# Row statistics of the input norm: sums of squares on TensorE from a ring of four buffers, with the tokens split at column 520

## The chip, the cores and the metric

The kernel runs on one core of a Trainium2 chip. The metric is device time in microseconds (us), the median of several executions; lower is better. The engines are TensorE (PE, with its weight loads PEld), VectorE (DVE), ScalarE (ACT), GpSimd (POOL) and SyncE (SP), which mostly issues DMAs.

## What is computed

One inference step of a one-layer hybrid decoder trunk: 1024 prompt tokens and 8 sample tokens share the weights, and 256 memory tokens have a projection of their own. The change is in the first norm, whose rows are the tokens:

```python
def rmsnorm(x, g):
    xf = x.astype(jnp.float32)
    y = xf * lax.rsqrt(jnp.mean(xf * xf, axis=-1, keepdims=True) + EPS)
    return (y * g.astype(jnp.float32)).astype(x.dtype)

z = rmsnorm(x, g) @ w_in          # prompt and sample tokens, in project()
z = rmsnorm(mem, g) @ w           # memory tokens, in memory_kv()
```

The columns of `z` feed four groups (forgetting attention, spatial gating, dilated attention, memory attention); then come the output projection, a residual add and a ConvFFN. All of that is untouched.

## The kernel before

The input lies transposed, features on the 128 partitions and tokens along the columns: 8 sample columns, then 1024 prompt columns (`COLS` = 1032), in `KC` = 8 chunks of 128 features. A product in full precision is made of three matmuls: both operands are split into a high and a low part (`hhi`, `hlo` for x times the gain; `whi`, `wlo` for the weights), and hi*hi, hi*lo and lo*hi are summed in PSUM (L903 to L905). ACT makes the high parts (`x_hi` L1228, `split_hi` L1220), DVE the low ones (`x_lo` L1622, `split_lo` L1616). The projection of x doesn't wait for the row statistics: 1/rms of a token is applied when the tile of `z` is moved out of PSUM.

The work of this stage is a list of units (L272): `(5, 0)` and `(5, 1)` are the two tiles of memory tokens against `w_mem`; then for each of five column blocks b of `w_in` come `(b, "S")`, whose first 8 columns are the sample tokens, and the eight prompt tiles `(b, 0)` to `(b, 7)`. A unit is 8 groups (kc) of three matmuls, 24 in all, and every engine's program walks the same list in its own order.

x comes in 24 pieces, i = 0 to 23, in three thirds of 8 (`xwhere` L296): memory tokens, the first 516 columns, the last 516. A piece is loaded by SP into one of seven slots (`x_load` L501; piece i waits until x_lo and the square of piece i-7 are done). ACT makes the high part (`x_hi`), and then the square of the piece (`x_square` L1236). For i = 0 to 15 ACT's order is x_hi(i), split_hi(i), x_square(i); pieces 16 to 23 come in `second_half` (L1263), which stands ahead of the eviction of unit (0,"S").

The statistics before: the square of the first piece of a third goes to `sacx`, the others go to `sqt0` and `sqt1` in turn, and POOL adds each of these to `sacx` (`x_add` L2314), 21 adds in all. A square waits until POOL has used the buffer (`x_acc`). When a third is complete, PE sums `sacx` over the partitions: a matmul per tile of 128 tokens, whose stationary operand is the 128x128 tile of `sacx` and whose moving operand is one column of ones (`stats` L816: 2, 4 and 5 matmuls, after units (5,0), (0,"S") and (0,2)). The second third also waits for `rtab` (made by `tables` L1592 on DVE) and for `st_cp`; with it go six small matmuls for the gains and then `page_transposes` (L834). DVE copies the sums out (`stat_copy` L1608) and POOL makes the inverse root (`inverse_rms` L2307, `rs_row`). POOL's own order is: 8 x_add, first inverse_rms, two indirect DMAs for `lfp`, a mask, 8 x_add, inverse_rms for tiles S, 0, 1, 2, 8 x_add, and from there two small instructions for each unit that is normed.

An eviction goes ACT square (L1312), DVE sum (L1672), POOL inverse root (L2310, L2313), DVE scale (L1685, L1692). DVE's `second_half` (L1638: copy of the sums, x_lo of pieces 16 to 23, a scan over `lft` L1647 and a subtraction L1649) stands in front of the eviction of (0,"S"). Prompt units take PSUM banks 0 to 3 in turn, so (0,4) waits for the eviction of (0,0), and so on. SP stores finished tiles (`outputs` L520); at unit (0,4) it waits for the normed sample rows, then moves q to `qb`, and then issues sixteen times two page loads for the key cache (`load_pages` L361), with the stores and the weight loads of the later blocks queued behind them.

Of the kernel before, what the change touches and what calls it, by code (L numbers as in the profile page):

```python
# [33 lines left out]
BLK = [(0, 512), (512, 260), (772, 512), (1284, 512), (1796, 512)]  # L34
ATT, DIL, MEMG = 0, 1, 2
NSET = 12

# [60 lines left out]
def build(nc, t):  # L98
# [5 lines left out]
    with ctx:  # L104
# [19 lines left out]
        u10_0 = cur[0]  # L124
# [44 lines left out]
        lft = at("lft", [P, 2, NH, P], f32, u10_0)[0]  # L169
        lmask = at("lmask", [P, 2 * NH * P], f32, pidx_end)[0]  # L170
        lscan = at("lscan", [P, 2 * NH * P], f32, 224416)[0]
        sqt1 = at("sqt1", [P, 516], f32, pidx_end + 4096)[0]
        rtab = at("rtab", [4, NR], f32, 224416)[0]
        relb = at("relb", [32, NH], f32, 224416 + 4608)[0]

# [22 lines left out]
        zs, o = at("zs", [NSAMP, 2308], f32, o)  # L198
        sA, o = at("sA", [P, 8, PAGES, NH], f32, o)
        accx = at("accx", [NSAMP, 2, NH, HD], f32, o - 4096)[0]  # L200
        sacx, sq_end = at("sacx", [P, COLS], f32, o - 4096)
        sqt0 = at("sqt0", [P, 516], f32, u10_0 + 4096)[0]
        lfp = at("lfp", [P, 2, PSZ * NH], f32, sq_end)[0]
        bias0 = o
        biasA, o = at("biasA", [P, 8, PAGES, NH], f32, o)
        oS = at("oS", [NSAMP, 4, WG], f32, bias0)[0]
        qb, o = at("qb", [P, 8, WG], f32, o)
        ring, o = at("ring", [P, 4, 4, WG], f32, o)
        x7 = at("x7", [P, 7, 516], f32, o - 16384)[0]
        coh = at("coh", [32, NR + 320], f32, bias0 + 4096 + 1024)[0]  # L210
        wost1 = at("wost1", [P, KC, P], f32, o)[0]
        wost0 = at("wost0", [P, KC, P], f32, u10_0)[0]
# [82 lines left out]

        def xwhere(i):  # L296

            c0, w = ((516, NMEM), (0, 516), (516, 516))[i // 8]
            return slice(c0, c0 + w), w, i % 8, 1 if i < 8 else 0

        def xslot(i):

            return x7[:, i % 7, 0:xwhere(i)[1]]

        def xsem(i):
            return S(f"x_ld{i % 7}")
# [484 lines left out]
        def _(pe):  # L791
# [10 lines left out]

            pe.wait_ge(S("const_ld"), 80)

            def stats(half):

                pe.wait_ge(S("x_acc"), 8 * half + 8)
                if half:
                    pe.wait_ge(S("rtab"), 4)
                    pe.wait_ge(S("st_cp"), half)  # L810
                cols = ([(9 + x, 516 + x * P) for x in range(2)],
                        [(0, 0)] + [(1 + tt, NSAMP + tt * P) for tt in range(3)],
                        [(1 + tt, NSAMP + tt * P) for tt in range(3, NT)])[half]
                if half == 1:

                    for j in range(3):  # L816
                        for r0 in (0, HD):
                            pe.matmul(ps[r0:r0 + HD, 7, 300 + j:301 + j], gq[0:1, 2 * j, :], ones[0:1, 0:1], start=True, stop=True)
                for x, c0 in cols:
                    m = pe.matmul(ps[:, 7, 288 + x:289 + x], sacx[:, c0:c0 + P], ones[:, 0:1], start=True, stop=True)  # L820
                m.then_inc(S("st_pe"), 1)

            def page_transposes():

# [49 lines left out]
            for u, k in enumerate(units):  # L874
# [13 lines left out]
                        pe.wait_ge(S("dve_z"), dve_last(pk))  # L888
                elif bank[k] in (2, 3):
                    pe.wait_ge(S("rtab"), 4)  # L890
                c0 = 0 if tt == "S" else (516 + tt * P if b == 5 else NSAMP + tt * P)
                for kc in range(KC):
                    if tt == "S" or (b == 5 and tt == 0):
                        pe.wait_ge(S("w_split"), POS[b] * KC + kc + 1)
                    if b == 0:
                        pe.wait_ge(S("x_split"), KC + kc + 1 if tt in ("S", 0, 1, 2) else 2 * KC + kc + 1)
                    if b == 5:
                        pe.wait_ge(S("x_split"), kc + 1)
                    sl = (POS[b] * KC + kc) % NW
                    w = WID[b]  # L900
                    lh, ll = hhi[:, kc, c0:c0 + P], hlo[:, kc, c0:c0 + P]
                    out = ps[:, bank[k], 0:w]
                    pe.matmul(out, lh, whi[:, sl, 0:w], start=(kc == 0), stop=False)  # L903
                    pe.matmul(out, lh, wlo[:, sl, 0:w], start=False, stop=False)  # L904
                    i = pe.matmul(out, ll, whi[:, sl, 0:w], start=False, stop=(kc == KC - 1))  # L905
                    if tt == NT - 1 or (b == 5 and tt == 1):
                        i.then_inc(S("w_used"), 1)
                    elif kc == KC - 1:
                        i.then_inc(S("z_done"), 1)
                if tt == NT - 1 or (b == 5 and tt == 1):  # L910

                    pe.wait_ge(S("w_used"), (POS[b] + 1) * KC)
                    pe.sem_inc(S("z_done"), 1)
                if k == (5, 0):
                    stats(0)
                if k == (0, "S"):
                    stats(1)
                    page_transposes()
                if k == (0, 2):
                    stats(2)  # L920
                if k == (0, 4):
                    page_sums()
                if k == (2, 1):
# [295 lines left out]
        def _(act):  # L1219
# [15 lines left out]

            def x_square(i):  # L1236

                c, w, kc, _ = xwhere(i)
                if kc == 0:
                    if i == 2 * KC:  # L1240
                        act.wait_ge(S("st_pe"), 1)
                    act.activation(sacx[:, c], xslot(i), ACT.Square).then_inc(S("x_sq"), 1)
                else:
                    if i >= 3:
                        act.wait_ge(S("x_acc"), i - 1)
                    act.activation((sqt0 if i % 2 else sqt1)[:, 0:w], xslot(i), ACT.Square).then_inc(S("x_sq"), 1)
            act.dma_start(relb[:, :], t["rel_bias"]).then_inc(S("tab_ld"), 16)
            act.dma_start(coh[:, :], t["coh"]).then_inc(S("tab_ld"), 16)
            act.dma_start(ca[:, :], t["ca"]).then_inc(S("const_ld"), 16)
# [34 lines left out]
            for u, k in enumerate(units):  # L1284
# [5 lines left out]
                r = rows(k)  # L1290
                rx = rsx[0:r, xi(k):xi(k) + 1]
                z = zview(k)
                act.wait_ge(S("rs_row"), 1 if b == 5 else 2 if u < UI[(0, 3)] else 3)
                act.wait_ge(S("z_done"), u + 1)
                dst = zdst(k)
                if b in COPY or b == 2:
# [281 lines left out]
        def _(dve):  # L1578
# [28 lines left out]

            def stat_copy(half):  # L1608

                a, b = ((9, 11), (0, 4), (4, 9))[half]  # L1610
                dve.wait_ge(S("st_pe"), half + 1)
                if half == 1:
                    dve.tensor_copy(ssx[:, 11:14], ps[:, 7, 300:303])
                dve.tensor_copy(ssx[:, a:b], ps[:, 7, 288 + a:288 + b]).then_inc(S("st_cp"), 1)
# [13 lines left out]
            for kc in range(KC):  # L1628
                x_lo(kc)
                split_lo(kc)  # L1630
            stat_copy(0)
            for kc in range(KC, 2 * KC):
                x_lo(kc)
                split_lo(kc)
            dve.wait_ge(S("const_ld"), 80)
# [667 lines left out]
        def _(pool):  # L2303
# [3 lines left out]
            def inverse_rms(out, src, width, done, value):  # L2307
# [3 lines left out]
                chain[0] += 1  # L2311
                pool.wait_ge(S("pool_chain"), chain[0])
                pool.tensor_tensor(out, out, nhalf[0:r, 0:n], ALU.pow).then_inc(S(done), 1)  # L2313
            def x_add(i):  # L2314

                c, w, _, _ = xwhere(i)
                pool.wait_ge(S("x_sq"), i + 1)
                if i % 8 == 0:
                    pool.sem_inc(S("x_acc"), 1)
                    return  # L2320
                if i % 8 > 1:
                    pool.wait_ge(S("x_acc"), i)
                pool.tensor_tensor(sacx[:, c], sacx[:, c], (sqt0 if i % 2 else sqt1)[:, 0:w], ALU.add).then_inc(S("x_acc"), 1)

            for i in range(KC):
                x_add(i)
            pool.wait_ge(S("st_cp"), 1)
            inverse_rms(rsx[:, 9:11], ssx[:, 9:11], DM, "rs_row", 1)
            pool.wait_ge(S("const_ld"), 80)
            for i in range(2):  # L2330
# [3 lines left out]

            pool.affine_select(out=wsT[:, :, :], in_=wsT[:, :, :], compare_op=ALU.is_ge, fill=0.0, base=0,
                               pattern=[[0, NH], [1, P]], channel_multiplier=-1).then_inc(S("ws_mask"), 2)
            for i in range(KC, 2 * KC):
                x_add(i)
            for u, k in enumerate(units):
                if k == (0, "S"):  # L2340
                    pool.wait_ge(S("st_cp"), 2)
                    inverse_rms(rsx[:, 0:4], ssx[:, 0:4], DM, "rs_row", 2)
                    for i in range(2 * KC, 3 * KC):
                        x_add(i)
                if k == (0, 3):
                    pool.wait_ge(S("st_cp"), 3)
                    inverse_rms(rsx[:, 4:9], ssx[:, 4:9], DM, "rs_row", 3)
# [98 lines left out]
```

## Time and profile before

| | |
|---|---|
| median of 3 runs | 1478.48 us |
| lowest, highest | 1466.24, 1486.55 us |
| the profiled execution | 1470.2 us, span of its instructions 1468.5 us |
| PE busy | 1402.7 us, 96% of the span |
| DVE busy | 942.8 us, 64% |
| ACT busy | 463.4 us, 32% |
| POOL busy | 186.3 us, 13% |
| mean granted TensorE clock | 0.965 of full speed |

Times in the rows are us from the span's start. The stage that the change touches is the first 100 us or so; the projections end near 297, attention near 520, and the rest is the output projection and the ConvFFN, where PE is busy nearly all the time.

### The profile page before, as it was taken

Reading aid. Unit: us, or ns where it says so; the run is one execution under the profiler, and the core shown is the slowest. Engines: PE = TensorE matmul, PEld = TensorE weight load, DVE = VectorE, ACT = ScalarE, POOL = GpSimd, SP = SyncE. Lnnn points to the kernel's source line nnn. Section 1 sums busy time; section 2 is a strip of 40 time slices with the busy share of each in tenths; the row PEclk is TensorE's granted clock in tenths of the full one; section 3 lists DMA queues with packets and bytes.
Section 4 is the critical chain, followed back from the end, with each engine's and each line's share of the span. In section 5 each row is a group of like instructions: output and inputs, shape, how many; then the busy total and the mean of one; then the engine's idle time right before and its main releaser. Section 6 shows DMA issues by size and latency. Waiting matters only on the chain.

```text
span 1468.5 us, 24237 instructions
## 1 busy us (share of the span) xinstructions
PE 1402.7 (96%) x8753; PEld 1271.9 (87%) x8753; DVE 942.8 (64%) x1412; ACT 463.4 (32%) x711; POOL 186.3 (13%) x245
## 2 busy tenths in 40 slices
PE   6899999969898999999999999999999999999999
PEld 4678887756665666899999999999999999999999
DVE  6758889876676685744765646556564746465654
ACT  6413121164455555522432222122222212121220
POOL 5540024332221243000000000000000000000000
PEclk9899999987888799999999999999999999999999
DMA  8248766687875776341001202020201102020203
GB/s 280 56 143 262 221 179 186 186 234 214 255 237 184 250 219 178 94 154 29 29 29 58 72 15 72 15 87 1 87 29 58 58 29 72 15 72 15 81 7 127
DMA packets 125536, 168.62 MB, mean 115 GB/s; under 512 B 22789, under 2 KB 99998, under 8 KB 125010
## 3 DMA queue, kind: packets, MB, share of 16 engines
q1 hardware_dynamic: 100988, 129.44, 28.6%
q0 software_dynamic: 7616, 22.03, 5.1%
q10 hardware_dynamic: 16814, 15.62, 3.5%
q8 instruction: 69, 1.13, 0.3%
q14 instruction: 49, 0.40, 0.1%
HBM read 153.09 MB, written 13.96 MB: 114 GB/s over the span
## 4 chain that ended last, share of the span: by engine, by line
PE 77%; DVE 9%; issue 4%; POOL 3%; DMA 2%; SPq 2%; ACT 1%; ACTq 1%; POOLq 0%; DVEq 0%
PE ps L1106 18%; PE ps L1105 18%; PE ps L1107 18%; PE ps L1003 4%; PE ps L1028 2%; PE ps L985 2%; PE ps L903 2%; PE ps L970 2%; PE ps L904 2%; PE ps L905 2%; POOL rsn L2313 1%; PE ps L969 1%; PE ps L1007 1%; PE ps L871 1%; DVE hlo L1625 1%
## 5 line engine op out<-in xcount | busy, mean ns | idle before, releaser
L1105 PE MATMUL ps<-hhi,uhi 128*128 128x344 f32 x1056 | 338.0, 320 | 0.0
L1106 PE MATMUL ps<-hlo,uhi 128*128 128x344 f32 x1056 | 336.5, 319 | 0.0
L1107 PE MATMUL ps<-hhi,ulo 128*128 128x344 f32 x1056 | 336.3, 318 | 0.0
L1105 PEld LDWEIGHTS ps<-hhi,uhi 128*128 128x128 f32 x1056 | 198.2, 188 | 0.5 <-issue 0.5
L1106 PEld LDWEIGHTS ps<-hlo,uhi 128*128 128x128 f32 x1056 | 198.2, 188 | 0.5 <-issue 0.5
L1107 PEld LDWEIGHTS ps<-hhi,ulo 128*128 128x128 f32 x1056 | 198.2, 188 | 0.0
L2222 DVE TENSOR_TENSOR uu<-ps,rstd_bc 128x1032 f32<-128x1032 f32 x44 | 54.2, 1233 | 202.4 <-PE ps L1107 202.2
L903 PE MATMUL ps<-whi,hhi 128*128 128x512 f32 (+1 forms) x376 | 145.9, 388 | 13.5 <-DVE wlo L1619 8.3
L1106 PE MATMUL ps<-alo,dhi 128*128 128x344 f32 x480 | 153.9, 321 | 0.0
L1107 PE MATMUL ps<-ahi,dlo 128*128 128x344 f32 x480 | 153.2, 319 | 0.0
L1105 PE MATMUL ps<-ahi,dhi 128*128 128x344 f32 x480 | 153.1, 319 | 0.0
L905 PE MATMUL ps<-whi,hlo 128*128 128x512 f32 (+1 forms) x376 | 143.1, 381 | 0.0
L904 PE MATMUL ps<-wlo,hhi 128*128 128x512 f32 (+1 forms) x376 | 142.7, 379 | 0.0
L2255 DVE TENSOR_TENSOR x<-ps,x 128x1032 f32<-128x1032 f32 x80 | 98.5, 1231 | 19.1 <-PE ps L1107 18.9
L1003 PEld LDWEIGHTS ps<-vst,pts 128*128 128x128 f32 x576 | 74.8, 204 | 30.5 <-issue 27.7
L903 PEld LDWEIGHTS ps<-whi,hhi 128*128 128x128 f32 x376 | 72.5, 193 | 31.7 <-DVE wlo L1619 12.3
L365 POOL DMA_DIRECT2D vring<-in_cache_a_v x128 | 70.0, 547 | 183.4 <-issue 143.5
L1523 ACT ACTIVATE convG<-uu,prm_a 128x1024 f32<-128x1024 f32 x22 | 27.4, 1244 | 201.9 <-DVE uu L2222 201.9
L1107 PEld LDWEIGHTS ps<-ahi,dlo 128*128 128x128 f32 x480 | 90.2, 188 | 0.0
L1105 PEld LDWEIGHTS ps<-ahi,dhi 128*128 128x128 f32 x480 | 90.1, 188 | 0.0
L1106 PEld LDWEIGHTS ps<-alo,dhi 128*128 128x128 f32 x480 | 90.1, 188 | 0.0
L1003 PE MATMUL ps<-vst,pts 128*128 128x65 f32 x576 | 82.9, 293 | 6.2 <-DVE oN L1960 5.9
(291 smaller groups left out, 2412.9 us busy)
## 6 DMA issues: line engine op xcount, KB each, us to landing
fst<-in_w_upL SPq DMA_DIRECT2D x44, 512.0 KB, 3.5
ring<-in_cache_a_k SPq DMA_DIRECT2D x168, 128.0 KB, 2.6
vring<-in_cache_a_v POOLq DMA_DIRECT2D x128, 128.0 KB, 3.3
vring<-in_cache_a_v SPq DMA_DIRECT2D x104, 128.0 KB, 3.0
ring<-in_cache_a_k ACTq DMA_DIRECT2D x88, 128.0 KB, 2.8
fst<-in_w_down SPq DMA_DIRECT2D x22, 512.0 KB, 3.5
wst<-in_w_in SPq DMA_DIRECT2D x32, 256.0 KB, 3.7
x<-in_xT SPq DMA_DIRECT2D x16, 258.0 KB, 3.7
```

What stands on the lines that cost most here:

```text
L365: sp.dma_start(dst[:, slot, j, :], pool[bass.ds(page, 1)].rearrange("o p c -> p (o c)"))\
L903: pe.matmul(out, lh, whi[:, sl, 0:w], start=(kc == 0), stop=False)
L904: pe.matmul(out, lh, wlo[:, sl, 0:w], start=False, stop=False)
L905: i = pe.matmul(out, ll, whi[:, sl, 0:w], start=False, stop=(kc == KC - 1))
L970: i = pe.matmul(out, q1c[0:K2, p, q0:q0 + P], klc[0:K2, p, c:c + w], start=False, stop=True)
L985: i = pe.transpose(ps[:, 4, j * P:(j + 1) * P], lg[:, g % 2, j * P:(j + 1) * P], ident)
L1003: i = pe.matmul(ps[:, 6, 0:HD + 1], pts[:, g % 2, j, :], vst[:, hp % 2, j, H % 2, :], start=(j == 0), stop=(j == nb - 1))
L1105: pe.matmul(out, lhs_hi(kc), rhs_hi(kc)[:, cs], start=(n == 0), stop=False)
L1106: pe.matmul(out, lhs_hi(kc), rhs_lo(kc)[:, cs], start=False, stop=False)
L1107: i = pe.matmul(out, lhs_lo(kc), rhs_hi(kc)[:, cs], start=False, stop=(n == nk - 1))
L2222: dve.tensor_tensor(c3(uu[:, :]), U3(k % 2), c3(rstd_bc[:, :]), ALU.mult).then_inc(S("f_free"), 1)
L2255: dve.tensor_tensor(c3(x2[:, d, :]), U3(d % 2), c3(x2[:, d, :]), ALU.add).then_inc(S("f_free"), 1)
```

## The change

Every square goes into one of four buffers (`sqt0`, `sqt1` and the two halves of a new `sqt2`, where `sacx` was), and PE sums each piece over the partitions as soon as it is there, accumulating over the eight pieces of a third in PSUM. POOL's adds are gone. `x_acc` is now counted by PE, once for each piece, and the square of piece i waits for the sums of piece i-4. The pieces of the first third are summed inside unit (5,0), behind each group of three matmuls; those of the second inside (0,"S"), the last behind it; those of the third behind (0,0), (0,1) and (0,2), 3, 3 and 2 pieces. The second third now is 520 columns (sample tokens and tiles 0 to 3) and the last one 512. So the sums of tile 3 come with the second third, and the wait for the third moves from (0,3) to (0,4). `stat_copy(0)` on DVE is moved behind two more pieces.

```diff
+XH = 520
-            c0, w = ((516, NMEM), (0, 516), (516, 516))[i // 8]
+            c0, w = ((XH, NMEM), (0, XH), (XH, COLS - XH))[i // 8]
+        def xsquare(i):
+            s4 = i % 4
+            return (sqt0, sqt1)[s4] if s4 < 2 else sqt2[:, s4 - 2]
...
-            def stats(half):
-                pe.wait_ge(S("x_acc"), 8 * half + 8)
-                if half:
+            def stats(i):
+                half = i // KC
+                cols = ([(9 + x, x * P) for x in range(2)],
+                        [(0, 0)] + [(1 + tt, NSAMP + tt * P) for tt in range(4)],
+                        [(1 + tt, NSAMP + tt * P - XH) for tt in range(4, NT)])[half]
+                if i % KC == 0 and half:
+                    pe.wait_ge(S("st_cp"), half)
+                if i == 2 * KC - 1:
                     pe.wait_ge(S("rtab"), 4)
...
+                pe.wait_ge(S("x_sq"), i + 1)
                 for x, c0 in cols:
-                    m = pe.matmul(ps[:, 7, 288 + x:289 + x], sacx[:, c0:c0 + P], ones[:, 0:1], start=True, stop=True)
-                m.then_inc(S("st_pe"), 1)
+                    m = pe.matmul(ps[:, 7, 288 + x:289 + x], xsquare(i)[:, c0:c0 + P], ones[:, 0:1],
+                                  start=(i % KC == 0 and x == cols[0][0]), stop=(i % KC == KC - 1 and x == cols[-1][0]))
+                m.then_inc(S("x_acc"), 1)
...
+                    if k == (5, 0):
+                        stats(kc)
+                    if k == (0, "S") and kc < KC - 1:
+                        stats(KC + kc)
...
-                if k == (5, 0):
-                    stats(0)
                 if k == (0, "S"):
-                    stats(1)
+                    stats(2 * KC - 1)
                     page_transposes()
-                if k == (0, 2):
-                    stats(2)
+                if b == 0 and tt in (0, 1, 2):
+                    for x in range(2 * KC + 3 * tt, min(2 * KC + 3 * tt + 3, 3 * KC)):
+                        stats(x)
...
             def x_square(i):
-                c, w, kc, _ = xwhere(i)
-                if kc == 0:
-                    if i == 2 * KC:
-                        act.wait_ge(S("st_pe"), 1)
-                    act.activation(sacx[:, c], xslot(i), ACT.Square).then_inc(S("x_sq"), 1)
-                else:
-                    if i >= 3:
-                        act.wait_ge(S("x_acc"), i - 1)
-                    act.activation((sqt0 if i % 2 else sqt1)[:, 0:w], xslot(i), ACT.Square).then_inc(S("x_sq"), 1)
+                w = xwhere(i)[1]
+                if i >= 4:
+                    act.wait_ge(S("x_acc"), i - 3)
+                act.activation(xsquare(i)[:, 0:w], xslot(i), ACT.Square).then_inc(S("x_sq"), 1)
...
-                act.wait_ge(S("rs_row"), 1 if b == 5 else 2 if u < UI[(0, 3)] else 3)
+                act.wait_ge(S("rs_row"), 1 if b == 5 else 2 if u < UI[(0, 4)] else 3)
...
-            stat_copy(0)
             for kc in range(KC, 2 * KC):
+                if kc == KC + 2:
+                    stat_copy(0)
                 x_lo(kc)
                 split_lo(kc)
...
-            def x_add(i):
-
-                c, w, _, _ = xwhere(i)
-                pool.wait_ge(S("x_sq"), i + 1)
-                if i % 8 == 0:
-                    pool.sem_inc(S("x_acc"), 1)
-                    return
-                if i % 8 > 1:
-                    pool.wait_ge(S("x_acc"), i)
-                pool.tensor_tensor(sacx[:, c], sacx[:, c], (sqt0 if i % 2 else sqt1)[:, 0:w], ALU.add).then_inc(S("x_acc"), 1)
-
-            for i in range(KC):
-                x_add(i)
```

The two other calls of `x_add` on POOL go too, and its inverse roots take columns 0 to 4 and 5 to 8 in place of 0 to 3 and 4 to 8; `stat_copy` does the same and waits for `x_acc` at 8, 16 and 24.

## Rows read from the trace of the kernel before

**Rows 1.** Waits of PE, 0 to 330: for whom, total, times, longest.
```profile
PE ps L903 <- DVE wlo L1619: 8.3, 6, 2.8
PE ps L871 <- DVE zo L1685: 4.6, 1, 4.6
PE ps L903 <- issue: 4.3, 1, 4.3
```
**Rows 2.** Timeline, POOL's adds and ACT's squares waiting: start, us, engine, line; idle before.
```profile
27.71 11.28 POOL L2323 TENSOR_TENSOR sacx<-sacx,sqt 128x516 f32<-128x516 f32 x7
29.05 0.64 ACT L1246 ACTIVATE sqt<-x 128x516 f32<-128x516 f32 x1 [4.43 <-POOL sacx L2323]
49.63 0.64 ACT L1246 ACTIVATE sqt<-x 128x516 f32<-128x516 f32 x1 [8.97 <-POOLq L2319]
```
**Rows 3.** Timeline, ACT's pace, and DVE's splits beside POOL's adds and after them.
```profile
31.25 0.71 ACT L1234 ACTIVATE hhi<-x,prm_a 128x516 fp32r<-128x516 f32 x1
32.91 0.71 ACT L1234 ACTIVATE hhi<-x,prm_a 128x516 fp32r<-128x516 f32 x1
34.40 1.77 DVE L1619 TENSOR_TENSOR wlo<-wst,whi 128x512 fp32r<-128x512 f32 x1
36.09 1.77 DVE L1625 SCALAR_TENSOR_TENSOR hlo<-x,prm_a,hhi 128x516 fp32r<-128x516 f32 x1
39.47 0.74 DVE L1625 SCALAR_TENSOR_TENSOR hlo<-x,prm_a,hhi 128x516 fp32r<-128x516 f32 x1
40.13 0.68 DVE L1619 TENSOR_TENSOR wlo<-wst,whi 128x512 fp32r<-128x512 f32 x1
```
**Rows 4.** Timeline of PE, the marks of its order.
```profile
12.23 0.80 PE L903 MATMUL ps<-whi,hhi 128*128 128x512 f32 x1
12.82 0.63 PE L904 MATMUL ps<-wlo,hhi 128*128 128x512 f32 x1
13.25 0.63 PE L905 MATMUL ps<-whi,hlo 128*128 128x512 f32 x1
26.96 0.47 PE L903 MATMUL ps<-whi,hhi 128*128 128x512 f32 x1 [0.30 <-PE ps L905]
44.73 1.19 PE L829 MATMUL ps<-ca,lfp 128*128 128x128 f32 x8
45.67 0.48 PE L903 MATMUL ps<-whi,hhi 128*128 128x512 f32 x1
75.07 0.77 PE L903 MATMUL ps<-whi,hhi 128*128 128x512 f32 x1 [4.25 <-issue]
83.07 1.02 PE L837 MATMUL ps<-lft,ca 128*128 128x512 f32 x2
86.11 0.79 PE L903 MATMUL ps<-whi,hhi 128*128 128x512 f32 x1
134.15 0.51 PE L903 MATMUL ps<-whi,hhi 128*128 128x512 f32 x1 [1.17 <-DVE wlo L1619]
```
**Rows 5.** Timeline of PE, what stands beside the one-column matmuls of L820.
```profile
20.23 0.40 PE L905 MATMUL ps<-whi,hlo 128*128 128x512 f32 x1
20.47 0.50 PE L820 MATMUL ps<-ca,sacx 128*128 128x1 f32 x4
20.83 0.48 PE L903 MATMUL ps<-whi,hhi 128*128 128x512 f32 x1
...
63.76 0.39 PE L905 MATMUL ps<-whi,hlo 128*128 128x512 f32 x1
63.99 1.17 PE L820 MATMUL ps<-ca,sacx 128*128 128x1 f32 x10
65.02 0.47 PE L903 MATMUL ps<-whi,hhi 128*128 128x512 f32 x1
```
**Rows 6.** Timeline, the chain from the eviction of (0,"S") to SP.
```profile
66.80 0.68 DVE L1672 TENSOR_REDUCE ssn<-sq 8x8 f32<-8x512 f32 x1 [0.80 <-ACT sq L1312]
83.37 0.32 SPq L536 DMA_DIRECT2D scr_q<-zo  x1
```
**Rows 7.** Stretches: us, PE busy (instructions), granted clock, DMA share, GB/s.
```profile
45.00:48.00 3.00, 3.00 (x15) 0.69 0.14 53
75.00:78.00 3.00, 2.93 (x7) 0.50 0.18 47
436.00:440.00 4.00, 4.00 (x27) 1.00 1.12 356
```
**Rows 8.** Timeline of PE in attention, narrow matmuls at either clock.
```profile
437.26 0.39 PE L976 MATMUL ps<-khh,qhl 128*128 128x256 f32 x1
437.57 0.38 PE L977 MATMUL ps<-klc,qhl 64*128 64x256 f32 x1
437.88 1.10 PE L1007 MATMUL ps<-vst,pts 128*128 128x65 f32 x8
454.75 1.97 PE L1007 MATMUL ps<-vst,pts 128*128 128x65 f32 x8
460.42 1.11 PE L1007 MATMUL ps<-vst,pts 128*128 128x65 f32 x8
```

More of the change, by code:

```diff
@@ L171, in build @@
         lscan = at("lscan", [P, 2 * NH * P], f32, 224416)[0]
-        sqt1 = at("sqt1", [P, 516], f32, pidx_end + 4096)[0]
+        sqt1 = at("sqt1", [P, XH], f32, pidx_end + 4096)[0]
         rtab = at("rtab", [4, NR], f32, 224416)[0]
@@ L200, in build @@
         accx = at("accx", [NSAMP, 2, NH, HD], f32, o - 4096)[0]
-        sacx, sq_end = at("sacx", [P, COLS], f32, o - 4096)
-        sqt0 = at("sqt0", [P, 516], f32, u10_0 + 4096)[0]
+        sqt2, sq_end = at("sqt2", [P, 2, XH], f32, o - 4096)
+        sqt0 = at("sqt0", [P, XH], f32, u10_0 + 4096)[0]
         lfp = at("lfp", [P, 2, PSZ * NH], f32, sq_end)[0]
@@ L208, in build @@
         ring, o = at("ring", [P, 4, 4, WG], f32, o)
-        x7 = at("x7", [P, 7, 516], f32, o - 16384)[0]
+        x7 = at("x7", [P, 7, XH], f32, o - 16384)[0]
         coh = at("coh", [32, NR + 320], f32, bias0 + 4096 + 1024)[0]
@@ L803, in _ @@
             pe.wait_ge(S("const_ld"), 80)
-            def stats(half):
-                pe.wait_ge(S("x_acc"), 8 * half + 8)
-                if half:
-                    pe.wait_ge(S("rtab"), 4)
[L810 to L814, printed above, removed]
+            def stats(i):
[6 more added lines that the diff above has]
+                if i == 2 * KC - 1:
+                    pe.wait_ge(S("rtab"), 4)
                     for j in range(3):
                         for r0 in (0, HD):
-                            pe.matmul(ps[r0:r0 + HD, 7, 300 + j:301 + j], gq[0:1, 2 * j, :], ones[0:1, 0:1], start=True, stop=True)
+                            pe.matmul(ps[r0:r0 + HD, 7, 300 + j:301 + j], gq[0:1, 2 * j, :], ones[0:1, 0:1], start=False, stop=False)
+                pe.wait_ge(S("x_sq"), i + 1)
                 for x, c0 in cols:
-                    m = pe.matmul(ps[:, 7, 288 + x:289 + x], sacx[:, c0:c0 + P], ones[:, 0:1], start=True, stop=True)
-                m.then_inc(S("st_pe"), 1)
+                    m = pe.matmul(ps[:, 7, 288 + x:289 + x], xsquare(i)[:, c0:c0 + P], ones[:, 0:1],
+                                  start=(i % KC == 0 and x == cols[0][0]), stop=(i % KC == KC - 1 and x == cols[-1][0]))
+                m.then_inc(S("x_acc"), 1)
             def page_transposes():
@@ L890, in _ @@
                     pe.wait_ge(S("rtab"), 4)
-                c0 = 0 if tt == "S" else (516 + tt * P if b == 5 else NSAMP + tt * P)
+                c0 = 0 if tt == "S" else (XH + tt * P if b == 5 else NSAMP + tt * P)
                 for kc in range(KC):
@@ L895, in _ @@
                     if b == 0:
-                        pe.wait_ge(S("x_split"), KC + kc + 1 if tt in ("S", 0, 1, 2) else 2 * KC + kc + 1)
+                        pe.wait_ge(S("x_split"), KC + kc + 1 if tt in ("S", 0, 1, 2, 3) else 2 * KC + kc + 1)
                     if b == 5:
@@ L1608, in stat_copy @@
             def stat_copy(half):
-                a, b = ((9, 11), (0, 4), (4, 9))[half]
-                dve.wait_ge(S("st_pe"), half + 1)
+                a, b = ((9, 11), (0, 5), (5, 9))[half]
+                dve.wait_ge(S("x_acc"), KC * (half + 1))
                 if half == 1:
@@ L2336, in _ @@
                                pattern=[[0, NH], [1, P]], channel_multiplier=-1).then_inc(S("ws_mask"), 2)
-            for i in range(KC, 2 * KC):
-                x_add(i)
             for u, k in enumerate(units):
@@ L2341, in _ @@
                     pool.wait_ge(S("st_cp"), 2)
-                    inverse_rms(rsx[:, 0:4], ssx[:, 0:4], DM, "rs_row", 2)
-                    for i in range(2 * KC, 3 * KC):
-                        x_add(i)
+                    inverse_rms(rsx[:, 0:5], ssx[:, 0:5], DM, "rs_row", 2)
                 if k == (0, 3):
                     pool.wait_ge(S("st_cp"), 3)
-                    inverse_rms(rsx[:, 4:9], ssx[:, 4:9], DM, "rs_row", 3)
+                    inverse_rms(rsx[:, 5:9], ssx[:, 5:9], DM, "rs_row", 3)
                 if k == units[NU - 1]:
```

## Prediction, made before the changed kernel was built or run

> **What bounds the kernel now.** The page gives PE 96% of the span, so the question for each stage is what keeps PE from starting its next unit. I read the waits of PE first, then the timeline around each wait, then the stretches for the granted clock. In the first 300 us PE stands still in three ways that could concern the change [rows 1]. It waits six times for the low part of the weights, 8.3 us in all, nearly all inside unit (0,"S"). It waits 4.3 us once for "issue": that is unit (0,4) at 75.07, held by the eviction of (0,0) [rows 4]. The 4.6 us at the end of the projections are one more eviction that is late, and belong to the stage behind.
>
> The first two have one root, POOL. Its seven adds of the second third take 11.28 us, and ACT's square of piece 11 stood 4.43 us behind them; the one of piece 18 stood 8.97 us behind POOL's place in its order [rows 2]. While POOL adds, DVE's splits take 1.77 us, and 0.74 and 0.68 us once it has stopped [rows 3]: DVE is slowed 2.4 times. So the reader should see two costs of the adds, the wait for them and the slowing of DVE beside them. From 75 us on PE waits only 1.17 us until the projections end, at 134.15 [rows 4], for weights that SP issued late. So two clocks run to that point: PE's own, and SP's, which starts with the store of (0,2) at 83.37 [rows 6].
>
> **What the change adds to PE.** The one-column matmuls are 11 now and become 16 + 40 + 32 = 88. Each is two instructions, since the rows count 10 for five. Ten of them between two neighbours of 0.23 us spacing cost 65.02 - 63.76 - 0.23 = 1.03 us, four cost 20.83 - 20.23 - 0.23 = 0.37 us [rows 5]. So one statistic is 0.206 us when five stand together and 0.185 us in pairs, and the 77 added ones cost near 77 x 0.2 = 15.6 us of PE time. Of them 14 lie in (5,0), 36 in (0,"S") and 27 behind (0,0) to (0,2).
>
> The Trainium skill ("TensorE: Matmul & The Clock Gate", section "Back-to-back issue gap") lists about 62 ns for a matmul of 1 to 64 columns when its firmware decodes it; an estimate by that is 154 x 0.062 = 9.5 us, some 6 us less than by the rows. The measured spacing here, 103 ns, has a weight load of 128 columns in front of every such matmul, so I go by the measurement.
>
> **What it removes, step by step, as PE's new timeline.**
> (5,0) starts at 12.2 as before. It ended at 20.47, with about 1.4 us of waits for DVE that disappear behind the added work: 19.1. Added are 8 x 0.37 = 3.0 us, and 0.5 us more because the first groups run at half speed (spacing 0.43 us [rows 4]): 22.6. The bare kernel was at 20.83 there [rows 5]; PE is 1.8 us late.
> (5,1) and the step to (0,"S") took 26.96 - 20.83 = 6.1 us [rows 4, 5]: (0,"S") starts at 28.7.
> (0,"S") now is 7 groups of 0.70 + 1.03 = 1.73 us and one of 0.70: 12.8 us, end at 41.5. It is no longer DVE that sets it: without POOL's adds a pair of splits is 0.74 + 0.68 = 1.4 us [rows 3], below 1.73. ACT is coupled to PE here: the square of piece 12 needs the sums of piece 8, which PE only makes at 29.7 + 1 us, so a wait of about 4 us stays on ACT, at another place, and pieces 13 to 15 then come at PE's pace. Queued behind that square are x_hi and split_hi of piece 13, which PE needs at 28.7 + 5 x 1.73 = 37.4; they are there by 33. The wait costs nothing.
> Behind it come the gain matmuls and the last five sums, 0.5 + 1.0 us, and the page transposes, 0.9 us (44.73 to 45.67 [rows 4]). DVE's tables, which ran 2.5 us behind its last split (40.8 to 43.3), now follow at about 36 and end by 39, and the page rows have long landed, since POOL issues them at about 25 to 29. (0,0) starts at 44.0, against 45.67: 1.6 us won.
> (0,0) to (0,2) took 18.3 us, of which 16.8 are 72 spacings of 0.233; the rest was half clock, 0.69 granted in 45:48 [rows 7]. Now 16.8 + 32 x 0.206 = 23.4 us: 67.4. (0,3) adds 5.6: 73.0, against 70.6 before. Here PE is 2.4 us behind.
> But the 4.3 us wait goes, and the half clock after it, 0.50 in 75:78 [rows 7], which cost about 2.2 us (11 spacings at 0.43 instead of 0.23). ACT's square 23 waits for the first sums behind (0,1), at 58.5, so the eviction of (0,"S") is summed at about 60.0 instead of 66.8 [rows 6]. With the pace of 4 us per unit as before, (0,0) is out at 68, five us before (0,4) asks for its bank. (0,4) takes 5.6 us and the page sums 3.05 (83.07 to 86.11 [rows 4]): (0,5) starts at 81.7 against 86.11 [rows 4]. PE is 4.4 us ahead.
> At 134.15 the 1.17 us wait also goes if SP is early enough. SP's chain starts with the store of (0,2), 6.8 us earlier by the same shift, so PE's 4.4 + 1.2 = 5.6 us is the smaller and decides.
>
> **Where I choose.** The sum is -5.6 us with full clock all along. The narrow stretch behind (0,"S"), 2.4 us of one-column matmuls and transposes, is there in both kernels, and the clock fell around it before (0.69 in 45:48 with PE busy 3.00 of 3.00 us [rows 7]). A fall costs about 1.6 us of dense matmuls. I count one, there or behind the sums of (0,0) or (0,1): -4 us. Against the profiled execution that is 1468.5 - 4 = 1464.5 us of span; the profiled run is 8 us below the median of the three, and against the median the forecast is 1478.5 - 4 = 1474.5 us. The costs that no row shows are small: the fourth buffer, the width 520 instead of 516 (below 1% of 0.7 us, 8 times), and the three inverse roots with one column moved. After the projections every queue starts from the end of the last unit, so the gain goes through; attention has DMA-fed waits whose phase can turn 2 us either way.
>
> **Rivals.**
> (A) The forecast: a small gain, -2 to -7 us. Chance 0.55.
> (B) The clock, on the other side. TensorE's clock falls to its lower level, 1.2 GHz, inside (0,"S"), where only 0.70 of each 1.73 us is wide matmuls. A group is then 3 x 0.43 + 10 x 0.2 = 3.3 us (narrow matmuls double too: eight of 65 columns took 1.97 us at the low and 1.11 at the high clock [rows 8]). Eight groups: 12.5 us more, net +7: 1485 us. For it: the fall at 45 to 48 with a busy PE. Against it: 436:440 in attention, granted 1.00 [rows 7], where four matmuls of 256 columns and eight of 65 alternate [rows 8], with no more wide work than here. It turns the sign when four of the eight groups run low. Chance 0.2.
> (C) A wash, within 2 us: the clock falls two or three times behind the blocks of sums, or DVE and POOL's ping-pong of evictions holds (0,4) anyway. About 1478 us. Chance 0.15.
> (D) The sums are cheaper than their rows. If the weight loads hid behind the wide neighbours, a sum of pairs would fall from 0.37 towards 0.12 us, and two thirds of 15.6 us would be back; ACT then binds at 1.66 us a piece (31.25 to 32.91 [rows 3]), and the gain is about -10 us: 1468. The skill's figure in the sentence above points this way, the two rows with neighbours against it. Chance 0.1.
> That leaves the case that POOL's adds were no cost, because ACT still waits for piece 12: it is in C, since DVE's slowing goes in any case.
>
> **How the numbers follow.** All cases lie within 1% of the time; 2% is 30 us, about what a measurement of this kernel can tell from no change, and no mechanism above reaches it in either direction. The runs before spread over 20 us, more than all cases, so the range is the cases widened by some of that: 1463 to 1486, which holds A to most of B. Faster by over 2%: 0.02, within 2%: 0.95, slower: 0.03.
>
> **What would show it.** Right: no POOL adds, splits of DVE at 0.7 us throughout, L903 in (0,"S") every 1.7 us without waits for wlo, a square of ACT waiting some 4 us for PE near 26 to 30, (0,4) with no wait near 73, (0,5) near 82, and the first wide matmul after 130 without a wait. Wrong: a granted clock of 0.5 between 29 and 42 (B); a wait for an eviction at (0,4) or (0,5) (C); a pair of sums well below 0.37 us (D); or a new wait for the weights in (0,"S") although POOL is idle, which would mean that DMA and not DVE was late.

## The result and the profile after

The changed kernel is slower: 1485.95 us (median of 21 runs) against 1471.91 us for the kernel before (21 runs). The ratio is 1.0075, with a 95% interval of 1.0044 to 1.0105; it leaves out the few slow executions of either kernel. By the ratio the loss is 11 us, by the two medians 14.0 us, in a direction that I gave one chance in five. The profiled execution has a span of 1490.9 us against 1468.5.

Where it goes can be read off three marks on PE, the starts of the page transposes (behind unit (0,"S")), of the page sums (behind (0,4)) and of the first key transposes (the end of the projections). They stand at 44.7, 83.1 and 284.7 us before, and at 60.4, 99.3 and 299.5 us after. The loss of 16 us is complete at the first mark, inside the stage that the change touches, and 14.8 us of it are left at the last. The other 7.7 us between the two profiled executions lie in attention (from the first key transposes to the output projection, 371.3 us after and 363.6 before). What comes behind attention takes 820.1 to 820.7 us in all profiles of this document.

The waits of PE, 0 to 330 us, beside [rows 1]:

```profile
PE ps L878 <- DVE zo L1691: 4.8, 1, 4.8
PE ps L1094 <- DVE nm L1943: 1.3, 1, 1.3
PE ps L995 <- ACT lg L1373: 0.7, 1, 0.7
PE ps L910 <- PE ps L912: 0.6, 2, 0.3
PE ps L910 <- DVE fa L1715: 0.3, 1, 0.3
PE ps L858 <- PE ps L912: 0.3, 1, 0.3
PE ps L910 <- DVE wlo L1624: 0.3, 1, 0.3
```

Both waits of the forecast are gone: 8.3 us for the low part of the weights have become 0.3, and unit (0,4) waits for nobody. A reader who went by waits alone would call this a success. The stretches tell the other half (us, PE busy and instructions, granted clock, DMA share, GB/s). Kernel after:

```profile
12.00:30.00 18.00, 18.00 (x62) 1.00 0.77 248
30.00:45.00 15.00, 14.70 (x73) 0.93 0.59 183
45.00:63.00 18.00, 18.00 (x79) 0.50 0.12 31
63.00:100.00 37.00, 37.00 (x185) 0.95 0.27 81
```

Kernel before, the same stretches:

```profile
12.00:30.00 18.00, 17.12 (x66) 1.00 0.93 304
30.00:45.00 15.00, 7.85 (x34) 0.66 0.45 138
45.00:63.00 18.00, 18.00 (x76) 0.91 0.24 68
```

PE is busy 18.00 of 18.00 us in 45:63, at half clock. The column for the clock says 1.00 for 12:30, although the spacing of the matmuls below is that of the low level; in the kernel before, too, it says 1.00 for 12:15, where the spacing is 0.43 us [rows 4]. So ahead of the first rise the level has to be read from the spacing. Timeline of PE after, a group of (5,0), a group of (0,"S") before the fall and one behind it:

```profile
19.03 0.77 PE L910 MATMUL ps<-whi,hhi 128*128 128x512 f32 x1
19.60 0.63 PE L911 MATMUL ps<-wlo,hhi 128*128 128x512 f32 x1
20.03 0.63 PE L912 MATMUL ps<-whi,hlo 128*128 128x512 f32 x1
20.46 0.85 PE L826 MATMUL ps<-ca,sqt 128*128 128x1 f32 x4
21.16 0.77 PE L910 MATMUL ps<-whi,hhi 128*128 128x512 f32 x1
...
37.99 1.17 PE L826 MATMUL ps<-ca,sqt 128*128 128x1 f32 x10
39.02 0.48 PE L910 MATMUL ps<-whi,hhi 128*128 128x512 f32 x1
...
43.76 2.13 PE L826 MATMUL ps<-ca,sqt 128*128 128x1 f32 x10
45.75 0.77 PE L910 MATMUL ps<-whi,hhi 128*128 128x512 f32 x1
46.32 0.63 PE L911 MATMUL ps<-wlo,hhi 128*128 128x512 f32 x1
46.75 0.63 PE L912 MATMUL ps<-whi,hlo 128*128 128x512 f32 x1
47.18 2.13 PE L826 MATMUL ps<-ca,sqt 128*128 128x1 f32 x10
49.16 0.77 PE L910 MATMUL ps<-whi,hhi 128*128 128x512 f32 x1
```

The spacing of the wide matmuls in (5,0) is 0.43 us, the lower level of 1.2 GHz, up to 32.4 us, well into (5,1); in the kernel before it became 0.23 us at about 15.4. So a group of (5,0) takes 21.16 - 19.03 = 2.13 us all the way. In (0,"S") ten narrow instructions cost 39.02 - 37.99 = 1.03 us at the high level, the term of my sum, and 45.75 - 43.76 = 1.99 us at the low one. The level falls at 43 and comes back at 63, in (0,0), where the wide matmuls stand alone again.

### The profile page after: what moved, and what is told of

The parts are those of the page before. It is cut to its first block, busy times and chain, and to the rows that moved or that the text cites. A ratio compares the mean times of both kernels' runs of the same rounds, so it can differ in the third digit from the quotient of the medians.

```text
span 1490.9 us, 24503 instructions
## 1 busy us (share of the span) xinstructions
PE 1436.5 (96%) x8907; PEld 1307.6 (88%) x8907; DVE 931.5 (62%) x1412; ACT 465.3 (31%) x711; POOL 158.0 (11%) x224
## 4 chain that ended last, share of the span: by engine, by line
PE 84%; DVE 7%; issue 4%; DMA 2%; POOL 1%; ACT 1%; ACTq 1%; SPq 0%; POOLq 0%; DVEq 0%
PE ps L1116 18%; PE ps L1115 18%; PE ps L1117 18%; PE ps L1013 4%; PE ps L910 4%; PE ps L911 3%; PE ps L912 3%; PE ps L1038 2%; PE ps L995 2%; PE ps L826 2%; PE ps L980 2%; PE ps L1017 1%; PE ps L979 1%; PE ps L878 1%; DVE ring L1663 1%
```

## The experiments

The marks of all profiles, in us, with the medians and the ratios to the kernel before on the same chip (that kernel's median was 1471.91 to 1479.44 us, by chip):

| kernel | page transposes | page sums | end of projections | median | ratio (95%) |
|---|---|---|---|---|---|
| before | 44.7 | 83.1 | 284.7 | | |
| after | 60.4 | 99.3 | 299.5 | 1485.95 | 1.0075 (1.0044 to 1.0105) |
| after_again | 59.8 | 100.7 | 300.8 | 1489.17 (a single execution) | |
| e1_block | 51.4 | 92.2 | 292.3 | 1488.23 | 1.0050 (1.0000 to 1.0100) |
| e2_filler | 55.8 | 93.3 | 293.4 | 1483.59 | 1.0061 (1.0025 to 1.0097) |
| e3_nosum | 36.3 | 67.5 | 267.7 | 1458.02 | 0.9892 (0.9852 to 0.9933) |
| e4_split | 46.4 | 80.7 | 283.3 | 1471.44 | 1.0016 (0.9977 to 1.0055) |
| e5_dve | 39.4 | 71.1 | 273.5 | 1469.12 | 0.9975 (0.9940 to 1.0011) |
| e5_again | 39.5 | 71.2 | 274.0 | 1469.34 | 0.9934 (0.9875 to 0.9992) |
| e6_f32r | 39.4 | 71.8 | 272.1 | 1459.34 | 0.9917 (0.9875 to 0.9959) |
| e6_again | 39.0 | 71.5 | 271.8 | 1478.14 (a single execution) | |
| e7_row | 36.9 | 70.5 | 271.6 | 1461.44 | 0.9917 (0.9879 to 0.9955) |
| e8_double | 59.9 | 100.5 | 300.8 | 1490.51 | 1.0054 (0.9999 to 1.0108) |

The marks repeat within 1.4 us between two executions of one kernel, the totals of one kernel scatter by 15 to 32 us. So mechanisms are judged by the marks and versions by the ratios.

Theory 1 is that the one-column matmuls between the wide ones cost twice: their own 0.1 us an instruction, and the clock of everything around them. Theory 2, the rival, is that the added instructions alone cost the time.

**e1_block, the sums of (5,0) behind the unit.**

```diff
+            buf = (sqt0, sqt1)[s4] if s4 < 2 else sqt2[:, s4 - 2]
+            return buf[:, 256 * (i // 4):256 * (i // 4) + 256] if i < KC else buf
...
-                if i >= 4:
-                    act.wait_ge(S("x_acc"), i - 3)
+                if i >= KC:
+                    act.wait_ge(S("x_acc"), max(KC, i - 3))
...
-                    if k == (5, 0):
-                        stats(kc)
...
+                if k == (5, 0):
+                    for x in range(KC):
+                        stats(x)
```

> The changed kernel, but the sums of the first third stand in one block behind unit (5,0) and not behind each of its groups (the four buffers hold two 256-column pieces each, so ACT is not held back). Same matmuls, same order of everything else. Theory 1 (the narrow matmuls between the wide ones keep TensorE at its low level in (5,0)): the clock rises near 15 us as in the kernel before, (5,0) with its sums ends near 23 instead of 29.7, (0,"S") starts near 29 instead of 37.2, (0,0) near 54 instead of 62.0, time some 8 us below the changed kernel. Theory 2 (the place of the sums is indifferent, the added instructions as such cost the time): (0,"S") starts at 37 as before, time unchanged.

Timeline of PE in e1_block:

```profile
17.07 0.63 PE L912 MATMUL ps<-wlo,hhi 128*128 128x512 f32 x1
...
18.04 0.40 PE L912 MATMUL ps<-wlo,hhi 128*128 128x512 f32 x1
...
20.37 0.39 PE L913 MATMUL ps<-whi,hlo 128*128 128x512 f32 x1
20.60 3.63 PE L827 MATMUL ps<-ca,sqt 128*128 128x1 f32 x32
24.08 0.48 PE L911 MATMUL ps<-whi,hhi 128*128 128x512 f32 x1
...
25.19 0.63 PE L911 MATMUL ps<-whi,hhi 128*128 128x512 f32 x1
```

With the same instructions, the wide ones first, the level is high from about 17.5 us. (5,0) with its sums ends at 24.1 instead of 29.7, and at the first mark the kernel is 9.0 us earlier than the changed one, at the last 7.2. That is theory 1 for (5,0). The rows show a second thing: behind the block of 32 narrow instructions the spacing goes back to 0.43 us, from 24.4 to 27.8 us. In (0,"S"), where the sums are still between the wide matmuls, the level is low again. The total doesn't show the gain: the median is no lower than that of the changed kernel, and the interval of its ratio, 1.0000 to 1.0100, holds both no loss and the loss of the changed kernel.

**e2_filler, more work.**

```diff
+                    if k in ((5, 0), (0, "S")):
+                        for _ in range(3):
+                            pe.matmul(ps[:, 4, 0:w], lh, whi[:, sl, 0:w], start=True, stop=True)
                     if k == (5, 0):
                         stats(kc)
```

> The changed kernel with three more 512-column matmuls in each group of (5,0) and (0,"S"), into a PSUM bank that nobody reads: 48 useless wide matmuls, 11.2 us at full clock. Theory 1 (clock): the level stays high in (0,"S") and rises early in (5,0); a group of (5,0) takes 1.77 us instead of 2.13, one of (0,"S") 2.43 instead of 3.41; (0,0) starts near 56 instead of 62.0, so the kernel with more work is 4 to 6 us faster than the changed one. Theory 2 (work): (0,0) starts 11 us later, near 73, and the time is 11 us longer.

The stretches of e2_filler:

```profile
30.00:45.00 15.00, 14.70 (x85) 1.00 0.60 185
45.00:63.00 18.00, 18.00 (x117) 1.00 0.30 84
```

and a group of its (5,0) (L915 are the fillers):

```profile
23.41 0.48 PE L910 MATMUL ps<-whi,hhi 128*128 128x512 f32 x1
23.73 0.40 PE L911 MATMUL ps<-wlo,hhi 128*128 128x512 f32 x1
23.97 0.39 PE L912 MATMUL ps<-whi,hlo 128*128 128x512 f32 x1
24.20 0.85 PE L915 MATMUL ps<-whi,hhi 128*128 128x512 f32 x3
24.89 0.50 PE L826 MATMUL ps<-ca,sqt 128*128 128x1 f32 x4
25.25 0.48 PE L910 MATMUL ps<-whi,hhi 128*128 128x512 f32 x1
```

Here 48 useless wide matmuls, 11.2 us at the high level, make the stage 4.6 us shorter at the first mark and 6.1 us at the last. A group of (5,0) is 1.84 us with six wide matmuls in it, and 2.13 with three. The rival of work alone would have put this kernel 11 us behind the changed one. It falls. ScalarE's squares wait for PE here as in the changed kernel (17.7 us from 12 to 63 us, against 22.1), so those waits don't hold the level low. The total doesn't tell this kernel from the changed one: 1.0061 and 1.0075, with intervals that overlap. The run also gives an estimate of what the change costs with the level high in (0,"S") and in most of (5,0): 293.4 - 11.2 = 282.2 us at the end of the projections, 2.5 us ahead of the kernel before.

**e3_nosum, the adds gone and nothing in their place.** 77 of the 88 sums are left out: the statistics are those of the last 128 features of each token only, with the divisor to match. What it computes is not the norm; only its time is of use.

```diff
+                if i % KC < KC - 1:
+                    pe.sem_inc(S("x_acc"), 1)
+                    return
...
-            inverse_rms(rsx[:, 9:11], ssx[:, 9:11], DM, "rs_row", 1)
+            inverse_rms(rsx[:, 9:11], ssx[:, 9:11], DM // 8, "rs_row", 1)
```

> The changed kernel without the one-column matmuls of the first seven pieces of each third (11 are left of 88): the row statistics are those of one eighth of the features, with the divisor to match. It shows what the removal of GpSimd's adds is worth when nothing takes their place. If my sum for the removed waits was right, ACT sets the pace at 1.66 us a piece, the last split of the second third is done near 32, (0,0) starts near 37, and the kernel is 10 to 14 us faster than the one before (ratio 0.990 to 0.993). If the adds' wait was hidden anyway, (0,0) starts near 45 and the time is that of the kernel before.

A little better than expected: page transposes at 36.3, 0.989 of the time. At the end of the projections it is 17.0 us ahead of the kernel before, more than the 12.6 us of waits in [rows 1]. The kernel before had the low level behind those waits, with 0.50 granted in 33:42 and in 75:78; here, from 15 to 102 us, only 36:42 is below 1.00 (0.62 and 0.81 in its two halves). So GpSimd's adds were worth removing. Against this kernel the 77 sums cost 299.5 - 267.7 = 31.8 us, twice the 15.6 us of the prediction.

**e4_split, the split alone.** The kernel before with `XH = 520`, the tile lists, `rs_row` and `stat_copy` as in the change.

```diff
-            c0, w = ((516, NMEM), (0, 516), (516, 516))[i // 8]
+            c0, w = ((XH, NMEM), (0, XH), (XH, COLS - XH))[i // 8]
...
-                act.wait_ge(S("rs_row"), 1 if b == 5 else 2 if u < UI[(0, 3)] else 3)
+                act.wait_ge(S("rs_row"), 1 if b == 5 else 2 if u < UI[(0, 4)] else 3)
```

> The kernel before with only the split at column 520 (pieces of 520 and 512 columns, tile 3 with the second third), GpSimd's adds as they were. Both theories: no difference, within 2 us, (0,0) at 45 to 46. If the split itself costs, for instance by a longer wait at (0,3) or (0,4), some of the 11 us shows here.

The ratio is 1.0016, no difference. The page transposes come 1.7 us later than in the kernel before, the page sums 2.4 us earlier and the end of the projections 1.4 us earlier. The split is not the cause of a loss of 16 us at the first mark.

**e5_dve, the adds on VectorE.** From the kernel before; `x_add` calls `dve` instead of `pool`, behind each `split_lo` and each `x_lo` of the last third, and `stat_copy(0)` moves behind one more `x_lo`.

```diff
             for kc in range(KC):
                 x_lo(kc)
                 split_lo(kc)
+                x_add(kc)
...
                 for i in range(2 * KC, 3 * KC):
                     x_lo(i)
+                    x_add(i)
```

> The kernel before with GpSimd's 21 adds moved to VectorE, nothing else: no narrow matmuls, TensorE as before. If what the adds cost before was GpSimd's order and VectorE slowed beside them, VectorE now needs 0.75 + 0.68 + about 0.7 us a piece, 2.1 us, against 3.4: the last split of the second third ends near 36 instead of 40.8, (0,0) starts near 41, the page sums start near 76 instead of 83, and the time is 5 to 8 us below the kernel before (ratio 0.995). If the gain of leaving the adds away came from VectorE having nothing to do, it is the time of before.

The marks are better than expected: page transposes at 39.4 and page sums at 71.1, 12 us ahead of the kernel before, with no work added to PE. The total showed little of it: 0.9975, no difference within its interval.

> The kernel of e5_dve once more. Its projections ended 11 us earlier than in the kernel before, but its median was only 4 us lower, and in its profile attention took 11 us longer at a lower granted clock. If that was the phase of the clock in attention, which differs between executions, the median ratio now lies nearer 0.993 and the stretch from the first key transposes to the output projection differs from 374.7 us by several us. If the earlier end of the projections itself makes attention slower, both come out as before.

The marks came out the same (39.5, 71.2, 274.0), and this time the ratio was 0.9934. The stretch from the first key transposes to the output projection was 370.8 us against 374.7, where the kernel before has 363.6. So part of the gain of 11 us at the end of the projections is missing in both profiles, and two profiles don't tell how much of that is the phase of the clock. The two ratios say 0.2 and 0.7%, and only the second is clear of its interval.

**e6_f32r, half as many narrow instructions.** From the changed kernel, with the squares and the ones of type fp32r; a memset makes the ones, and `stat_copy` reads every second column.

```diff
-                    m = pe.matmul(ps[:, 7, 288 + x:289 + x], xsquare(i)[:, c0:c0 + P], ones[:, 0:1],
+                    m = pe.matmul(ps[:, 7, 320 + 2 * x:322 + 2 * x], xsquare(i)[:, c0:c0 + P], onesr[:, 0:2],
```

> The changed kernel with the squares written in the type fp32r, so that a one-column sum is one instruction with one weight load and not two (the moving operand has two columns of ones). 88 narrow instructions instead of 176, in the same places. Theory 1 (clock): with half the narrow work between the wide matmuls the high level is reached earlier in (5,0) and kept longer in (0,"S"); (0,0) starts near 46 instead of 62.0 and the page sums near 85 instead of 99. Theory 2 (work alone): each of the 88 saves 0.1 us, 9 us in all, (0,0) at 56, with the level low in the same stretches.

Stretches and timeline of e6_f32r:

```profile
30.00:45.00 15.00, 14.80 (x96) 1.00 0.42 131
45.00:63.00 18.00, 18.00 (x96) 1.00 0.30 89
```

```profile
18.54 0.28 PE L828 MATMUL ps<-onesr,sqt 128*128 128x2 f32 x2
18.68 0.48 PE L912 MATMUL ps<-whi,hhi 128*128 128x512 f32 x1
...
28.98 0.39 PE L914 MATMUL ps<-whi,hlo 128*128 128x512 f32 x1
29.22 0.61 PE L828 MATMUL ps<-onesr,sqt 128*128 128x2 f32 x5
29.69 0.48 PE L912 MATMUL ps<-whi,hhi 128*128 128x512 f32 x1
```

The level is high from 18.5 us on and never falls in (0,"S"). The page transposes come 21.0 us earlier than in the changed kernel, where the 88 instructions that are gone would account for 9. The kernel beats the one before, 0.9917 (0.9875 to 0.9959), and so the changed one. Both marks came earlier than either theory's number.

> The kernel of e6_f32r once more, one look. In its first profile attention took 381.9 us from the first key transposes to the output projection, the longest of all profiles, though its median was among the lowest. If the stretch differs by execution, it comes out nearer 364 to 374 here, with the projections ending at the same 272 us.

The marks repeat (39.0, 71.5, 271.8). The expectation for attention failed: the stretch to the output projection was 384.5 us, after 381.9 in the first profile, the two longest of all, though the median of this kernel is among the lowest. The granted clock of 300:520 was 0.77 and 0.76 in them, against 0.83 in the kernel before. Why attention is so long in these two executions (1475.81 and 1478.14 us against a median of 1459.34) stays open.

**e8_double, the narrow instructions back.** e6_f32r with each sum made twice; the sum that is read then has `start=False`.

```diff
+                    pe.matmul(ps[:, 7, 400 + 2 * x:402 + 2 * x], xsquare(i)[:, c0:c0 + P], onesr[:, 0:2],
+                              start=(i % KC == 0 and x == cols[0][0]), stop=False)
```

> The e6_f32r kernel with every narrow sum made twice (the second copy goes to columns that nobody reads): 176 narrow instructions again, as in the changed kernel, but of the type fp32r. Theory 1 (clock, by the amount of narrow work between wide matmuls): the level stays low in (5,0) and falls in (0,"S") as in the changed kernel; (0,0) starts at 55 to 62 and the page sums near 95, far more than the 88 x 0.1 = 9 us of added work. Theory 2 (work alone): 3 to 9 us more than e6_f32r, (0,0) at 44 to 49, page sums near 80. If the type and not the amount holds the level low, theory 2's times come with a high level throughout.

Stretches of e8_double, and a group of its (5,0):

```profile
45.00:63.00 18.00, 18.00 (x78) 0.50 0.12 35
```

```profile
20.59 0.77 PE L914 MATMUL ps<-whi,hhi 128*128 128x512 f32 x1
21.16 0.63 PE L915 MATMUL ps<-wlo,hhi 128*128 128x512 f32 x1
21.59 0.63 PE L916 MATMUL ps<-whi,hlo 128*128 128x512 f32 x1
```

This is the sharpest pair of the study. 88 instructions of 0.1 us, some 9 us, put the end of the projections back by 300.8 - 272.1 = 28.7 us, and the low level is where it is in the changed kernel: in all of (5,0), and in 45:63. Against e6_again, which ran on the same chip, it is 29.0 us. The type of the matmul is not the cause, nor are the buffers, which are the same in both; it is how much narrow work stands between the wide matmuls. Whether the number of narrow instructions counts or the time they take, these runs don't separate.

**after_again.**

> The changed kernel once more, one look. Theory 1 has the low level in (5,0) and in (0,"S") as a property of the kernel: (0,0) starts at 60 to 63 again. If the level there is chance, a run of the same code should show it high in one of the two, and (0,0) 5 to 15 us earlier.

59.8, 100.7, 300.8 us, and 0.50 in 45:63 again. The low level came with the kernel both times, and is not chance.

**e7_row, sums as a row.** The ones are the stationary operand and the squares the moving one. Each piece is one wide matmul, and a small one for the last 8 of 520 columns, which add to a row of sums in PSUM; the row is copied out, and 11 small matmuls behind (5,1), (0,0) and (0,2) turn it into columns. GpSimd's first inverse root moves behind its page loads, and the last third is summed 4 and 4 pieces at a time.

```diff
+                m = pe.matmul(ps[0:RW, 7 if third == 1 else 4, 0:w1], onesr[:, 0:RW], xsquare(i)[:, 0:w1], start=a, stop=z_)
+                if w > 512:
+                    m = pe.matmul(ps[0:RW, 4, 310:310 + w - 512], onesr[:, 0:RW], xsquare(i)[:, 512:w], start=a, stop=z_)
+                m.then_inc(S("x_acc"), 1)
...
+                    m = pe.matmul(ps[:, 7 if third else 5, 288 + x:289 + x], xrow[:, c0:c0 + P], ones[0:1, 0:1],
```

> A version that should beat both: the sums of squares on TensorE with the ones as the stationary operand and the squares as the moving one, so each piece is one matmul of 256 or 512 columns (and a small one for the last 8 of 520) that accumulates a row in PSUM, 24 wide matmuls in place of 88 narrow ones. The row is copied out, and 11 one-element-deep matmuls turn it into columns once a third is complete. By theory 1 the level stays high all through; a group of (0,"S") is 0.70 + 0.3 us, so ScalarE sets the pace at 1.66 us. (0,0) near 38 to 40, page sums near 71, time 10 to 16 us below the kernel before, close to the kernel without the sums (ratio 0.989 to 0.993). If work on TensorE of any form was the cost, it lands near the changed kernel.

Timeline of PE in e7_row, a group of (0,"S"):

```profile
31.86 0.40 PE L929 MATMUL ps<-whi,hlo 128*128 128x512 f32 x1
32.09 0.40 PE L823 MATMUL ps<-sqt,onesr 128*2 128x512 f32 x1
32.33 0.17 PE L825 MATMUL ps<-sqt,onesr 128*2 128x8 f32 x1
32.36 0.47 PE L927 MATMUL ps<-whi,hhi 128*128 128x512 f32 x1
```

A piece costs 32.36 - 32.09 = 0.27 us of PE instead of 1.03, and the clock stays. The page transposes come at 36.9, 0.6 us behind the kernel that leaves the sums out. Ratio 0.9917 (0.9879 to 0.9955), 11 us below the median of the kernel before, as expected. It and e6_f32r can't be told apart by their times.

## Why the prediction was wrong

The steps, in the order of the prediction.

- The first failed step is the first line of the new timeline: (5,0) ends at 22.6. It ended at 29.7. I took the rise of the clock at about 15.4 us over from the kernel before, and priced the narrow matmuls at the low level for the first groups alone, 0.5 us. With four narrow instructions behind each three wide ones the level didn't rise in the unit at all: 8 groups of 2.13 us. e1_block gives 5.6 of the 7.1 us back by moving the same instructions.
- (0,"S"), 12.8 us, took 20.2 (37.2 to 57.4): three groups at 1.81 us, where my sum had 1.73, and from 43 us on 3.41 us a group. That was my rival B with its 3.3 us, to which I gave 0.2. The evidence that I set against it, narrow work in attention at 1.00 [rows 8], was of another mixture: in the kernel before, from 438.83 to 441.90, eight matmuls of 65 columns take 0.94 of 3.07 us, where the one-column ones take 1.03 of 1.81. The row that I held for B, 0.69 in 45:48 with a busy PE [rows 7], stands right behind one-column matmuls and transposes, and should have weighed more. It doesn't prove B, since PE had also just waited 0.84 us:

```profile
43.37 0.51 PE L818 MATMUL ps<-ca,prm_b 1*64 1x1 f32 x12 [0.84 <-issue]
43.81 1.05 PE L820 MATMUL ps<-ca,sacx 128*128 128x1 f32 x8
```

- B's total, 1485 us, is close to the median, but by luck. B had 12.5 us more in (0,"S") and nothing in (5,0); (0,"S") took 7.4 us more than in my sum, and (5,0) ended 7.1 us later. And both B and the range start from 1478.5 us, the median of three executions, where 21 gave 1471.91: B put the change at +7 us, and +11 to +14 were measured. That the range, 1463 to 1486, just holds 1485.95 is luck too.
- The last sums and the transposes were to take 2.4 us and took 4.6 (57.4 to 62.0), at the low level; (0,0) to (0,2) took 26.1 us for 23.4, with a low stretch at 80 to 84.
- The price of the sums at the high level was nearly right: 1.03 us for five up to the next wide matmul, as forecast. But the wide matmul behind them takes 0.32 us to the next one and not 0.23 (23.41 to 23.73 in e2_filler), 0.09 us in each group, which the sum left out. The Trainium skill ("TensorE: Matmul & The Clock Gate", section "Back-to-back issue gap") has 62 ns for such a matmul, as the prediction says; the measured spacing is 103 ns here, and in e6_f32r, with 29.69 - 28.98 - 0.23 = 0.48 us for five, 96 ns.
- The removed costs were right in kind: no wait for weights, none at (0,4), DVE's splits at 0.69 to 0.76 us throughout. ACT's square of piece 12 did wait for PE, 7.1 us instead of 4, and PE never waited for ACT in the projections. Their worth was 17.0 us by e3_nosum.
- With the level high in the two units my sum nearly stands: the first mark of e2_filler less its 11.2 us of filler is 44.6, where I had 43.1 for it (16 groups with 0.09 us left out make 1.4 us of the difference), and the end of the projections is 2.5 us ahead, where I had 4 with one fall of the clock. e2_filler has that one fall, behind the sums of (0,1): 0.50 in 75:78.

So the balance at the end of the projections has three terms. GpSimd's adds gone and nothing in their place: -17.0 us (e3_nosum against the kernel before). The 77 sums with the level high in the two units: 282.2 - 267.7 = +14.5 us (e2_filler without its filler, against e3_nosum). The level of the clock: 299.5 - 282.2 = +17.3 us. Together they are the +14.8 us. The 11.2 us of filler in it are an estimate, 48 spacings of 0.233 us; the first three fillers still ran at the low level (13.64 to 14.92 us), so the last two terms can shift against each other by some 0.6 us. The pair of e6_f32r and e8_double supports the last term: there it is 28.7 - 88 x 0.1 = 20 us. Of attention's 7.7 us the second profile of the changed kernel shows 3.0 (366.6 us); with stretches of 363.6 to 384.5 us over all profiles, these runs can't say whether any of it belongs to the change.

## What to carry to other kernels

Price a narrow matmul by its measured spacing (here 0.10 us an instruction at the high level and 0.20 at the low one) and by what it does to the clock of its wide neighbours; the second can be the larger. If sums over partitions must be fed in between matmuls, make the data the moving operand and the ones the stationary one, or at least halve the number of instructions. And when a change makes every wait of TensorE vanish and the kernel isn't faster, look at the spacing of equal matmuls before looking for a wait.

## What the runs showed of the hardware

- A busy TensorE can be a slow one. In the changed kernel it had no gap above 0.3 us from 12.6 to 63 us and ran at 1.2 GHz for (5,0) and for the second half of (0,"S"), 0.50 with PE busy 18.00 of 18.00. The Trainium skill ("TensorE: Matmul & The Clock Gate", section "What's actually happening") says that the clock is set by how busy the PE has been recently. If busy is read as the profile's busy time, this trace doesn't agree.
- Adding wide matmuls made a stage shorter (e2_filler, 4.6 us at the first mark), with the level high in 45:63 where it had been 0.50.
- While GpSimd adds, VectorE's splits take 2.4 times as long [rows 3]. With VectorE doing the same adds itself the page sums came 12 us earlier (e5_dve).
- The scatter of the totals within one kernel goes with the mean granted clock: the changed kernel's executions reach from 1474.91 us at 0.972 to 1507.15 us at 0.948, some 13 us for 0.01. In the profiles of all kernels the part behind attention is the same within 0.6 us, and attention differs by up to 21 us.
